# Routed rows of a mixture of experts: spread by TensorE, or written to memory and fetched per token

## The reference

```python
top_logits, top_idx = lax.top_k(logits, TOP_K)          # 2 of 8
top_gates = jax.nn.softmax(top_logits, axis=-1)
for e in range(N_EXPERTS):
    out = out + gates[..., e:e + 1] * swiglu(x, w_gu[e], w_down[e])
x = layer_norm(DEEPNORM_ALPHA * x + ffn, ln2_g[layer], ln2_b[layer])
```

## Time and profile before

| what | us |
|---|---|
| runs (three) | 1794.58, 1795.94, 1796.08; median 1795.94 |
| profiled execution, first to last instruction (span) | 1792.3 |
| median of the runs over that span | 3.6 |
| busy in the span | PE 1772.3, DVE 1385.4, ACT 1080.7, POOL 139.4 |
| expert 0's first matmuls to the last spread | about 1004 to 1781 |

### The profile page before, as it was taken

The page is one execution under the profiler, slowest core; times in us unless marked ns, Lnnn a source line. Parts: engine busy times, 40 slices in busy tenths (PEclk is TensorE's granted clock), DMA queues, the critical chain, the costliest instruction groups (busy, mean ns, idle before and its releaser), DMA issues.

```text
span 1792.3 us, 26725 instructions
## 1 busy us (share of the span) xinstructions
PE 1772.3 (99%) x11347; PEld 1595.9 (89%) x11347; DVE 1385.4 (77%) x1634; ACT 1080.7 (60%) x1207; POOL 139.4 (8%) x142
## 2 busy tenths in 40 slices
PE   9999999999999999999999999999999999999997
PEld 8999999999988999998998888888888888888885
DVE  6895588577665766655687899988889898889897
ACT  7754455455534354444445787776777777777774
POOL 1454260000000100000120000000000000000000
PEclk9999999999999999999999999999999999999999
DMA  9341454656546645665462799999998999899993
GB/s 285 118 119 60 135 171 141 218 170 200 186 167 200 207 158 165 204 219 174 140 223 85 262 373 378 348 335 372 354 374 310 375 351 378 307 380 347 379 368 133
DMA packets 263592, 442.15 MB, mean 247 GB/s; under 512 B 11254, under 2 KB 135641, under 8 KB 263337
## 3 DMA queue, kind: packets, MB, share of 16 engines
q1 hardware_dynamic: 263464, 440.36, 70.8%
HBM read 436.89 MB, written 1.06 MB: 244 GB/s over the span
## 4 chain that ended last, share of the span: by engine, by line
PE 93%; DVE 4%; ACT 2%; issue 1%; DMA 0%; SPq 0%; DVEq 0%; ACTq 0%
PE bank L429 28%; PE bank L427 28%; PE bank L428 27%; DVE ring_r L417 1%; PE bank L3233 1%; PE bank L3150 1%; ACT hi_ring L402 1%; PE bank L2518 1%; PE bank L1344 1%; PE bank L1336 1%; DVE arena L919 1%; PE bank L1828 1%; PE bank L3357 0%; PE bank L2148 0%; PE bank L3358 0%
## 5 line engine op out<-in xcount | busy, mean ns | idle before, releaser
L417 DVE TENSOR_TENSOR ring_r<-ring,hi_ring 128x2048 fp32r<-128x2048 f32 x401 | 905.6, 2284 | 249.8 <-ACT hi_ring L402 249.8
L402 ACT CAST hi_ring<-ring 128x2048 fp32r<-128x2048 f32 (+1 forms) x404 | 757.5, 1903 | 140.0 <-PE bank L429 133.4
L427 PE MATMUL bank<-hi_ring,arena_r 128*128 128x512 f32 (+1 forms) x1526 | 568.9, 373 | 0.7 <-DVE ring_r L417 0.7
L428 PE MATMUL bank<-ring_r,arena_r 128*128 128x512 f32 (+2 forms) x1534 | 567.5, 370 | 0.0
L429 PE MATMUL bank<-hi_ring,arena_r 128*128 128x512 f32 (+1 forms) x1526 | 566.4, 371 | 0.0
L427 PE MATMUL bank<-ring_r,hi_ring 128*128 128x256 f32 (+1 forms) x1400 | 399.3, 285 | 0.0
L429 PE MATMUL bank<-ring_r 128*128 128x256 f32 (+1 forms) x1400 | 395.7, 283 | 0.0
L428 PE MATMUL bank<-ring_r,hi_ring 128*128 128x256 f32 (+1 forms) x1400 | 395.5, 283 | 0.0
L427 PEld LDWEIGHTS bank<-hi_ring,arena_r 128*128 128x128 f32 x1526 | 286.8, 188 | 52.5 <-DVE ring_r L417 2.4
L428 PEld LDWEIGHTS bank<-ring_r,arena_r 128*128 128x128 f32 (+1 forms) x1534 | 287.9, 188 | 51.0
L429 PEld LDWEIGHTS bank<-hi_ring,arena_r 128*128 128x128 f32 x1526 | 286.9, 188 | 50.3
(11 more groups left out here) (422 smaller groups left out, 1620.0 us busy)
## 6 DMA issues: line engine op xcount, KB each, us to landing
ring<-in_w_gu_moe SPq DMA_DIRECT2D x176, 1024.0 KB, 6.2
ring<-in_w_down_moe SPq DMA_DIRECT2D x88, 1024.0 KB, 5.3
ring<-in_w_in SPq DMA_DIRECT2D x31, 1024.0 KB, 5.7
ring<-in_w_gu_dense SPq DMA_DIRECT2D x22, 1024.0 KB, 5.2
ring<-in_w_up SPq DMA_DIRECT2D x16, 1024.0 KB, 5.4
ring<-in_w_down SPq DMA_DIRECT2D x16, 1024.0 KB, 5.1
ring<-in_w_in_a SPq DMA_DIRECT2D x10, 1024.0 KB, 5.8
ring<-in_w_down_dense SPq DMA_DIRECT2D x10, 1024.0 KB, 5.0
```

Of the source, the lines that this page charges most:

```text
L402: q.e.copy(hi_ring[:, b:b + m], ring[:, a:a + m]).then_inc(*q.did(("hi", of.tag, i)))
L417: q.e.tensor_tensor(ring_r[:, a:a + m], ring[:, a:a + m], hi_ring[:, b:b + m].bitcast(F32), ALU.subtract).then_inc(*q.did(("lo", of.tag, i)))
L427: q.e.matmul(ps, a[0], b[0], start=first, stop=False)
L428: q.e.matmul(ps, a[0], b[1], start=False, stop=False)
```

## The change

The rows of experts 0 to 6 are no longer scaled, split and spread by PE. ACT copies them from PSUM to one of two buffers (`rows_out`), POOL writes them to a tensor `done` in memory (7 x 128 rows, and one row of zeros). POOL and DVE work out, for each token and each of its two experts, the row of `done` where it lies; a token of expert 7, or one with a place above 128, gets the row of zeros. After expert 6 POOL issues four indirect fetches of 128 rows (two halves of the tokens, first and second expert), two buffers (`home`) in turn, and DVE adds them to `acc` in column groups 2 to 5 of expert 7's up part, times the token's gate. Expert 7's rows take the old way, so that one turned place matrix and one column of gates remain in the main round. The round `over` is as it was. The diff, with blank lines and one hunk (the same new argument of `emit`) left out:

```diff
@@ -222,10 +222,11 @@
         posi = sb("posi", [P, SEQ], I32)
         ix = sb("ix", [P, 2, 8], U32)
         flag = sb("flag", [P, 1], I32)
+        gi = sb("gi", [P, 4], U32)
         bank = [ctx.enter_context(nc.psum_tensor(f"bank{i}", [P, 512], F32)) for i in range(8)]
         counts = Counts()
-        plays, banks = emit(A, cst, out, sem, counts, off, arena, arena_r, ring, ring_r, hi_ring, C, vec, sm, posi, ix, flag, bank)
+        plays, banks = emit(A, cst, out, sem, counts, off, arena, arena_r, ring, ring_r, hi_ring, C, vec, sm, posi, ix, flag, gi, bank)
         idle = Idle()
         for play in plays:
             play(idle)
@@ -591,6 +592,9 @@
     lparts, lmv, linv = at(9128, 24), at(9152, 4), at(9156, 2)
     wsum, wbias, shift = small(8), small(8), small(2)
     ye = pair_at(0, 1024)
+    rows_out = [at(0, 1024), at(1024, 1024)]
+    home = [at(23192, 1024), at(24216, 1024)]
+    slots, late_, which, sums = at(25240, 2, 8), at(25256, 2, 8), at(25272, 2, 2, 8), at(25304, 2, 2)
     fin, last_gb, last_sq = at(13824, 2, 1024), at(10648, 2, 1024), at(4096, 1024)
     vx4 = vx.rearrange("p a (h d) -> p a h d", d=65)
     alpha = float(4 ** 0.25)
@@ -3137,7 +3141,7 @@
                     q.wait_ge(("xt" if part else "xthi", c, k // 4))
                     src = (xt[c].hi, xt[c].lo)[part]
                     t = q.e.matmul(ps[:, 0:2 * P], src[:, k * P:(k + 1) * P], pm[:, c, :], start=(part + c == 0), stop=(part + c == 2))
-            t.then_inc(*q.did(("ps", "w", "xs", 0, k)))
+            t.then_inc(*q.did(("ps", "w", "xs", 0, k), *([("pmused", "w", 0)] if k == 7 else [])))
     def pe_pick(q, R, x):
         q.wait_ge(("pm", R.tag, x))
@@ -3148,12 +3152,15 @@
                     q.wait_ge(("yt", c, k // 4))
                     src = (xt[c].hi, xt[c].lo)[part]
                     t = q.e.matmul(ps[:, 2 * P * part:2 * P * (part + 1)], src[:, k * P:(k + 1) * P], pm[:, c, :], start=(c == 0), stop=(c == 1))
-            t.then_inc(*q.did(("ps", R.tag, "xs", x, k)))
+            t.then_inc(*q.did(("ps", R.tag, "xs", x, k), *([("pmused", R.tag, x)] if k == 7 and not spreads(R, x) else [])))
+
+    def spreads(R, x):
+        return [y for y in range(2) if R is over or x + y == 7]
     def pe_pick_places(q, R, x):
         pf = pm.bitcast(F32)
         q.wait_ge(("ge", 0), ("ge", 1))
-        for y in range(2):
+        for y in spreads(R, x):
             ps = R.banks.take(q, R.tag, "st", x + y)
             for c in range(2):
                 q.e.transpose(ps[:, c * P:(c + 1) * P], pf[:, c, P * y:P * y + P], ident)
@@ -3201,7 +3208,7 @@
             R.banks.drop((R.tag, "xs", x, k), ("xs", R.tag, x, k))
     def dve_pick_gates(q, R, x):
-        for y in (x, x + 1):
+        for y in [x + y for y in spreads(R, x)]:
             q.wait_ge(("st", R.tag, y))
             q.e.tensor_copy(gs[:, y:y + 1], R.banks(R.tag, "st", y)[:, SEQ:SEQ + 1]).then_inc(*q.did(("gs", R.tag, y)))
             R.banks.drop((R.tag, "st", y), ("gs", R.tag, y))
@@ -3217,9 +3224,9 @@
             q.e.copy(xs2.hi[:, k, :], R.banks(R.tag, "xs", x, k)[:, 0:2 * P]).then_inc(*q.did(("xshi", R.tag, x, k)))
     def act_pick_places(q, R, x):
-        for y in (x, x + 1):
+        for y in [x + y for y in spreads(R, x)]:
             q.wait_ge(("ps", R.tag, "st", y))
-            if y >= 4:
+            if y >= 4 and R is over:
                 q.wait_ge(("spread", R.tag, y - 4))
             q.e.copy(ST[y % 4], R.banks(R.tag, "st", y)[:, 0:SEQ]).then_inc(*q.did(("st", R.tag, y)))
@@ -3291,6 +3298,8 @@
                 dve_turn(q, R, x, 4 * j - 4)
             elif x == 0:
                 dve_pick_gates(q, R, 0)
+            if R is main and x == 7 and j > 1:
+                dve_home(q, j - 2)
     def pe_down_half(q, R, x, f0, hf, ps):
         i = R.w.at["down", x, f0]
@@ -3325,11 +3334,21 @@
             act_high(q, R.w.at["down", x, f0] + 2, R.w)
             if f0 == 2:
                 act_turn(q, R, x, 20)
+        if R is main and x < 7:
+            if x < 2:
+                q.wait_ge(("y", "a1", 1, 1))
+            else:
+                q.wait_ge(("out", "done", x - 2))
+            for hf in range(2):
+                q.wait_ge(("ps", R.tag, "down", x, hf))
+                q.e.copy(rows_out[x % 2][:, 512 * hf:512 * hf + 512], R.banks(R.tag, "down", x, hf)).then_inc(*q.did(("rows out", x, hf)))
+                R.banks.drop((R.tag, "down", x, hf), ("rows out", x, hf))
+            return
         q.wait_ge(("gs", R.tag, x))
-        if x:
+        if R is main:
+            q.wait_ge(("out", "done", 5), ("out", "done", 6))
+        elif x:
             q.wait_ge(("spread", R.tag, x - 1))
-        elif R is main:
-            q.wait_ge(("y", "a1", 1, 1))
         for hf in range(2):
             q.wait_ge(("ps", R.tag, "down", x, hf))
             q.e.activation(ye.hi[:, 512 * hf:512 * hf + 512], R.banks(R.tag, "down", x, hf), ACT.Copy, scale=gs[:, x:x + 1]).then_inc(*q.did(("yehi", R.tag, x, hf)))
@@ -3381,6 +3402,50 @@
         for hf in range(2):
             dve_spread_half(q, R, x, hf)
+    def pool_slots(q):
+
+        q.wait_all("layer1")
+        q.e.memset(home[0][0:1, :], 0.0).then_inc(*q.did(("zeros",)))
+        q.wait_ge(("zeros",))
+        q.e.dma_start(A["done"][7 * P:7 * P + 1, :], home[0][0:1, :]).then_inc(*q.landed("out_zeros", ("out", "zeros")))
+        q.wait_ge(("place", 0), ("place", 1))
+        q.e.tensor_scalar(late_, posm, float(P), 8.0 * P, ALU.is_gt, ALU.mult).then_inc(*q.did(("late",)))
+        for c in range(2):
+            q.e.tensor_scalar(slots[:, c, :], cc("iota8"), float(P), -1.0, ALU.mult, ALU.add).then_inc(*q.did(("first", c)))
+        q.wait_ge(("late",), ("first", 0), ("first", 1))
+        q.e.tensor_tensor(late_, late_, posm, ALU.add).then_inc(*q.did(("late", "place")))
+        q.wait_ge(("late", "place"))
+        q.e.tensor_tensor(slots, slots, late_, ALU.add).then_inc(*q.did(("slots",)))
+        q.wait_ge(("slots",))
+        q.e.tensor_scalar(slots, slots, 7.0 * P, None, ALU.min).then_inc(*q.did(("slots", "kept")))
+        q.wait_ge(("slots", "kept"))
+        for c in range(2):
+            for y in range(2):
+                q.e.tensor_tensor(which[:, c, y, :], oh[:, c, y, :], slots[:, c, :], ALU.mult).then_inc(*q.did(("which",)))
+
+    def dve_slots(q):
+        q.wait_ge(("which",))
+        q.e.tensor_reduce(sums, which, AX, ALU.add).then_inc(*q.did(("slot",)))
+        q.wait_ge(("slot",))
+        q.e.tensor_copy(gi[:, :], sums.rearrange("p c y -> p (c y)")).then_inc(*q.did(("gi",)))
+
+    def pool_homes(q):
+
+        for x in range(7):
+            q.wait_ge(("rows out", x, 0), ("rows out", x, 1))
+            q.e.dma_start(A["done"][x * P:x * P + P, :], rows_out[x % 2]).then_inc(*q.landed(f"out_done{x % 2}", ("out", "done", x)))
+        q.wait_ge(("gi",), ("out", "zeros"), ("out", "done", 5), ("out", "done", 6))
+        for n in range(4):
+            if n > 1:
+                q.wait_ge(("homed", n - 2))
+            q.e.indirect_dma_start(out=home[n % 2], out_offset=None, in_=A["done"], in_offset=bass.IndirectOffsetOnAxis(ap=gi[:, n:n + 1], axis=0)).then_inc(*q.landed(f"in_home{n % 2}", ("in", "home", n)))
+
+    def dve_home(q, n):
+        c, y = divmod(n, 2)
+        q.wait_ge(("in", "home", n), *([("homed", n - 1)] if y else [("acc", "w", c, hf, -1) for hf in range(2)]))
+        ends = [("acc", "w", c, hf, 6) for hf in range(2)] if y else []
+        q.e.scalar_tensor_tensor(out=acc[:, c, :], in0=home[n % 2], scalar=gt2[:, c, y:y + 1], in1=acc[:, c, :], op0=ALU.mult, op1=ALU.add).then_inc(*q.did(("homed", n), *ends))
+
     def pe_experts(q, R):
         if R is main:
             pe_pick_normed(q)
@@ -3390,7 +3455,7 @@
             pe_up(q, R, x)
             if x == 0 and R is main:
                 look(q)
-            if x:
+            if x and R is over:
                 pe_spread(q, R, x - 1)
             if x % 2 and x < 7:
                 pe_pick(q, R, x + 1)
@@ -3431,7 +3496,8 @@
             dve_up(q, R, x, rows)
             if x == 0 and R is main:
                 look(q)
-            if x:
+                dve_slots(q)
+            if x and R is over:
                 dve_spread(q, R, x - 1)
             if x % 2 and x < 7:
                 dve_pick(q, R, x + 1)
@@ -3650,6 +3716,8 @@
         q.stage("layer1")
         pool_layer1(q)
         q.stage("moe")
+        pool_slots(q)
+        pool_homes(q)
         q.mark("experts")
         look(q)
         beside(q, pool_rest)
@@ -3729,6 +3797,7 @@
     arrays["in_table"] = table
     cst = nc.dram_tensor("in_table", table.shape, F32, kind="ExternalInput").ap()
     aps["rows"] = nc.dram_tensor("rows", (16, P), F32).ap()
+    aps["done"] = nc.dram_tensor("done", (7 * P + 1, 1024), F32).ap()
     out = nc.dram_tensor("out_0", (1, SEQ, 1024), F32, kind="ExternalOutput").ap()
     program(nc, aps, cst, out)
     r = run_bass_kernel_spmd(nc, [arrays], core_ids=[0])
```

2 lines of the change are left out of this document (1 added, 1 removed).

## The result

The changed kernel takes 1778.09 us against 1796.01 us, medians of four runs each; the ratio is 0.9904 with a 95% interval from 0.989 to 0.9917. Timed again beside the kernel before, with five runs, it takes 1779.84 against 1794.59 us, ratio 0.9922 (0.9908 to 0.9936). In the last group of runs two executions of the kernel before, at 2929 and 1902 us, had a granted clock of 0.56 and 0.87, and no ratio counts them. The forecast was 1779.5 us, range 1777 to 1787.

What follows compares the result with a forecast made beforehand. PE was taken to bound the expert stage; 13.65 + 3.0 + 0.2 - 0.4 = 16.45 us off the 1792.3 us span gives 1775.9, plus 3.6 around it 1779.5 us, range 1777 to 1787.

Steps and rivals of the forecast that it cites:

- (a): PE's spreading of experts 0 to 6 between up and down parts goes: 7 x 1.95 = 13.65 us off.
- (b): PE's turned place matrices ahead of experts 2, 4 and half of 6 go: 2.5 x 1.21 = 3.0 us off.
- (c): Pair of place matrices in expert 0's first column group goes: 0.2 us off, as PE waits for DVE; range 0 to 1.2.
- (d): ACT and DVE lose additions and copies, about 8 us of DVE per expert pair: worth nothing itself, lets PE's savings count.
- (g): Four fetches of 512 KB and four DVE additions, at most 1.5 us each, in expert 7's up part: hidden.
- (h): Added DMA traffic of 5.8 MB: weight loads later but hidden, just so in expert 7; 0.4 us allowed, shared with index arithmetic.
- (i): POOL's newly used queue may add to start or end, outside the span: -0.5 to +3.6 us, taken as 0.
- The 3.6 us: Time around the trace's span: median 1795.94 us is 3.6 above span 1792.3; the same added to the new span 1775.9.
- The ceiling: Rival: DMA limit in the expert stage; at 370 GB/s 1783 us; chance 0.13 together with refill; below 364, slower, 0.03.
- The refill: Rival: ACT or DVE late at picks or in expert 7, 3 to 9 us back, 1783 to 1788; 0.13 together with ceiling.
- The late fetches: Rival: slow POOL issue makes DVE's additions in expert 7's up part wait; PE loses from T = 13.6 us; chance 0.05.
- the prediction's other case: If DVE's 2.3 us tensor_tensor locked POOL out, each fetch issue would wait one of them: T = 8.6 us, still hidden.

Runs made afterwards that it cites:

- e1: Changed kernel, but PE turns all place matrices and picks all gates again, with ACT's and DVE's copies: 1782.88 us, ratio 0.9935 to the kernel before.
- e9: Changed kernel plus four value-neutral 128x512 DVE operations after the up parts of experts 2 to 6, where the spreads' additions stood: 1788.08 us, ratio 0.9964.
- e3: Changed kernel without the four fetches, buffers filled with zeros once; writes and the four DVE additions stay: 1778.71 us, ratio 0.9907.
- e4: Changed kernel with the rows of experts 0 to 6 written three times, 7.3 MB more traffic: 1779.94 us, ratio 0.9909.
- e2: Changed kernel without writes, index arithmetic, fetches and the four additions; ACT still copies the rows out: 1778.8 us, ratio 0.9906.
- e5: Changed kernel with all four fetches into one buffer, each issued only after DVE used the one before: 1784.84 us, ratio 0.9941.
- e6: Changed kernel with each of the four additions cut in two halves, one behind the conversions of each side: 1778.91 us, ratio 0.9907.
- e8: Changed kernel with halved additions, and place matrices of experts 2 and 3 built behind expert 0's fifth column group: 1776.93 us, ratio 0.9899.
- e12: Changed kernel with halved additions, late place matrices, and gate operations of ACT and DVE moved to expert 0's down part: 1777.91 us, ratio 0.9909.

## Why the prediction was right, step by step

*(a) and (b), the spreads and the matrices.* 16.65 us forecast, 16.45 measured as steps. e1 parts them: 13.2 for the spreads (13.65 forecast), 3.2 for the matrices (3.0). The slots read from start to start were right to 0.05 us for a spread and 0.1 for a pair of matrices.

*(c), expert 0.* 0.2 forecast; measured -0.1 against one trace of the kernel before and 0.15 against the other. That PE would only wait longer was right; the wait came in two places, 0.80 and 0.54 us, together 1.34 where the prediction named 1.4.

*(d), DVE's relief.* "Worth nothing by itself; it is what lets (a) and (b) count" was right, and it was more than a remark: e9 takes DVE's relief away at five of the seven boundaries, and 7.2 us are gone. What I then expected of e9 was wrong. I had read the idle time of DVE in front of L417 (20.5 us in the earlier trace rows) as slack; it is waiting for ACT, which waits for PE, and it isn't at the boundary. The margin that counts is between DVE's end and PE's need there, 0.7 us at expert 2's boundary.

*(g) and (h), additions and traffic.* The 0.4 us allowed were too little, 1.2 measured, and for the wrong cause: the step that failed is that DVE "stays below full". It does on average, but each addition of 1.27 us (at most 1.5 forecast) falls behind a product and a split where only 0.25 us are idle, and the down part runs without a gap. That the transfers themselves are hidden was right (e3, e4), and e4's landings of up to 13.6 us stayed within the budget of 11.4 + 4.4 us for a late load.

*(i), what lies outside the span.* Taken as 0, and close: on record are time and span of most runs, and they differ by 2.1 to 2.3 us in every run of the kernel before, by 1.8 in every run of the changed kernel. So 0.4 us go there; in e2, which has no transfers by POOL, the difference is 2.1 to 2.2 again, in e9 2.6 to 2.9. Why is open. (It is also why e2's and e9's medians are higher than their traces suggest.) The 3.6 us were no measure of it; they joined one execution's span to the median of others.

*The total.* The gain from the first pick to the end was forecast as 16.45 us and is 15.2, 1.25 too much. The 3.6 us around the span were 1.8, 1.8 too much. That the new span was forecast to 0.2 us (1775.9, measured 1776.1) is in part luck: the first pick of that trace came 1.1 us earlier than in the one before. And that the time came out 1.4 us from the first median owes something to the same scatter.

*The signs.* The boundaries, the wait in expert 0, the four matmuls each on L3378 and L3379 and additions that never wait came as named. The weights' landings did not stay under 11 us (11.5 at worst). Two signs of being wrong were seen as well. PE waits behind L418 in expert 7, 0.4 us in two waits: that is the step named under (g). And the last fetches landed more than 35 us after expert 6's last eviction (1666.70 in that trace), being issued 38 and 49 us after it, and were still in time; this sign forgot that they wait for their buffers, which (g) itself had counted.

*The rivals.* The ceiling falls with e4. By the HBM Reference of the Trainium skill (section Specifications (TRN2)), a core's share is about 358 GB/s, and one that streams alone has more; the window of e4 has 379 GB/s for 740 us on this one core, so for a lone core only the higher figure holds. The refill did not come, but e9 shows that it was one edit away. The late fetches did not come: T was 7.1 us for a write and 8.6 us for a fetch. These are POOL's two lines in the kernel after, issue time (min, median, max, in ns) and landing in us:

```profile
L3436 POOL DMA_DIRECT2D done<-arena x7: 531/531/656, 1095.7 to 1667.8; - x7
...
DMA to landing us min/median/max: 6.0/7.1/7.9
```

```profile
L3441 POOL DMA_INDIRECT arena<-done,gi x4: 1833/2528/2747, 1675.5 to 1715.7; - x4
...
DMA to landing us min/median/max: 8.0/8.6/9.3
```

The price of a late fetch was mis-sized: the 4 us of cover that I gave DVE do not exist there, and PE pays for the stall and then for the lower clock (e5). In one buffer T = 9.4 us was enough to lose 5.9 us. The prediction's 13.6 us are for two buffers and no run tests them; in the changed kernel the last fetch has 16.9 us from its issue to its use.

By the SBUF — State Buffer page of the Trainium skill (section Who interferes with whom), a DVE tensor_tensor does not hold up POOL's descriptors, but with both inputs in SBUF it contends with what GpSimd reads there; the prediction used the first half. The writes can't test it: all seven are issued while DVE is idle. The fetches are issued beside DVE's long tensor_tensor, and their issue is held up by it. These are the first fetches of e5 and e9, each with the row of DVE under way (the 4.49 us are two operations back to back, of which the first ends at about 1676.1):

```profile
1675.62 1.45 POOL L3441 DMA_INDIRECT arena<-done,gi  x1 [8.02 <-DMA done<-arena]
1673.88 4.49 DVE L418 TENSOR_TENSOR ring_r<-ring,hi_ring 128x2048 fp32r<-128x2048 f32 x2 [1.00 <-ACT hi_ring L403]
...
1684.54 2.70 POOL L3441 DMA_INDIRECT arena<-done,gi  x1 [6.77 <-DMA done<-arena]
1684.04 2.29 DVE L418 TENSOR_TENSOR ring_r<-ring,hi_ring 128x2048 fp32r<-128x2048 f32 x1 [1.00 <-ACT hi_ring L403]
```

The issue takes 1.45 us where it starts 0.5 us ahead of the operation's end, and 2.70 where it starts 1.8 ahead: it ends 0.9 us behind that end in both. The ten traces with fetches agree. Of their 40 issues 33 start while such a conversion is the only operation under way, and end 0.8 to 1.0 us after it; the third and fourth fetches of e6, e8 and e12 start beside an operation of 0.68 us and take 0.94 us. No run issues a fetch beside an idle DVE, so what the issue takes by itself isn't shown. So the prediction's other case came true, each issue waits for the operation under way, and T came out at its 8.6 us; as it said, that is still hidden.

## What to carry to other kernels

Work taken from the busiest engine counts by its slots only as far as the next engine is relieved at the same place: look at the margin between that engine's last result and the need for it there, not at its busy share or its total idle time. A round trip through memory is free where its due time is a whole expert away, and its cost is the operation that takes the data in, so cut that in pieces that fit the gaps. Compare kernels from a common point in the trace when the stages ahead of the change scatter more than the change is worth.
